# A two-layer hybrid decoder trunk in split fp32: key and query projections paired like the feed-forward, and the order of work at the head and at the stage borders

## The reference

```python
for l in range(DEPTH):          # DEPTH = 2
    x = x + 0.5 * rmsnorm(swiglu(rmsnorm(x, g1), w_gate, w_up, w_down), g2)      # D_FF = 2816
    x = x + rmsnorm(hybrid_mixer(rmsnorm(x, g3), cos, sin, w_in, ...), g4)       # retention + gated linear attention
    x = x + rmsnorm(memory_cross_attn(rmsnorm(x, g5), rmsnorm(mem, g6), w_q, w_kv, w_o), g7)
    x = x + 0.5 * rmsnorm(swiglu(rmsnorm(x, g8), w_gate2, w_up2, w_down2), g9)

def memory_cross_attn(h, mem_n, w_q, w_kv, w_o):       # 4 heads of 256, 256 memory tokens
    q = (h @ w_q).reshape(bsz, t, XA_HEADS, XA_DH)
    k, v = jnp.split(mem_n @ w_kv, 2, axis=-1)
    s = jnp.einsum('bthd,bmhd->bhtm', q, k) * (XA_DH ** -0.5)
    return (softmax(s) @ v) @ w_o
```

## Time and profile before

| | |
|---|---|
| median of three executions | 1198.43 us |
| the profiled execution's own time | 1198.46 us |
| its span, first to last instruction | 1196.6 us |
| PE busy | 1187.7 us, 99% |
| weight loads (PEld), beside PE | 1017.4 us, 85% |
| DVE busy | 821.2 us, 69% |
| ACT busy | 693.0 us, 58% |
| GpSimd busy | 147.5 us, 12% |
| mean granted TensorE clock | 0.999 |
| DMA | 217.84 MB, 182 GB/s over the span |

### The profile page before, as it was taken

How to read it: one execution, slowest core, us unless ns; L and a number is a source line. 1 busy time by engine, 2 the same in 40 slices (tenths; PEclk the granted TensorE clock), 3 DMA queues, 4 the chain that set the end, 5 groups by cost and what they waited for, 6 DMA issues and landing times.

```text
span 1196.6 us, 17899 instructions
## 1 busy us (share of the span) xinstructions
PE 1187.7 (99%) x6492; PEld 1017.4 (85%) x6492; DVE 821.2 (69%) x1258; ACT 693.0 (58%) x1190; POOL 147.5 (12%) x230
## 2 busy tenths in 40 slices
PE   9999999999999999999999999999999999999998
PEld 8788888779898888888888888887899988888886
DVE  6766645788667677775487875477887676778752
ACT  7655445756565566664466764376566565666641
POOL 3000002573100100000000000025531001000000
PEclk9999999999999999999999999999999999999999
DMA  9656565454444455556465555554545444555550
GB/s 371 224 183 217 182 205 186 150 211 142 163 172 162 138 193 184 203 187 209 152 207 181 201 198 194 193 200 139 172 140 178 161 151 159 185 205 177 192 178 36
DMA packets 33063, 217.84 MB, mean 182 GB/s; under 512 B 3920, under 2 KB 4176, under 8 KB 9440
## 3 DMA queue, kind: packets, MB, share of 16 engines
q1 hardware_dynamic: 32848, 216.77, 53.0%
q10 hardware_dynamic: 144, 0.13, 0.0%
HBM read 215.84 MB, written 1.05 MB: 181 GB/s over the span
## 4 chain that ended last, share of the span: by engine, by line
PE 95%; DMA 2%; DVE 1%; ACT 1%; issue 1%; POOL 0%; SPq 0%; POOLq 0%; DVEq 0%; ACTq 0%
PE acc L558 21%; PE acc L559 21%; PE acc L560 21%; PE acc L716 16%; PE acc L717 9%; PE tb L619 2%; DMA raw<-in_gu 2%; PE mb L795 1%; DVE w_lo L1466 1%; ACT w_hi L1049 1%; PE mb L560 0%; PE mb L559 0%; PE mb L558 0%; PE mb L882 0%; PE mb L866 0%
## 5 line engine op out<-in xcount | busy, mean ns | idle before, releaser
L1466 DVE SCALAR_TENSOR_TENSOR w_lo<-raw,first,w_hi 128x512 fp32r<-128x512 f32 x576 | 413.4, 772 | 87.4 <-ACT w_hi L1049 85.8
L1049 ACT ACTIVATE w_hi<-raw,first 128x512 fp32r<-128x512 f32 x568 | 367.6, 714 | 112.5 <-PE acc L717 47.0
L716 PE MATMUL acc<-xT,w_hi 128*128 128x512 f32 x864 | 300.2, 392 | 0.0
L717 PE MATMUL acc<-xT,w_lo 128*128 128x256 f32 x864 | 242.5, 281 | 0.0
L558 PE MATMUL acc<-w_hi,xT 128*128 128x512 f32 x592 | 235.8, 398 | 1.0 <-DVE xT L1472 0.9
L559 PE MATMUL acc<-w_lo,xT 128*128 128x512 f32 x592 | 231.2, 391 | 0.0
L560 PE MATMUL acc<-w_hi,xT 128*128 128x512 f32 x592 | 231.1, 390 | 0.0
L716 PEld LDWEIGHTS acc<-xT,w_hi 128*128 128x128 f32 x864 | 161.8, 187 | 35.1
L1458 DVE TENSOR_TENSOR w_lo<-raw,w_hi 128x1024 fp32r<-128x1024 f32 x112 | 124.6, 1146 | 90.0 <-ACT w_hi L1043 89.4
L717 PEld LDWEIGHTS acc<-xT,w_lo 128*128 128x128 f32 x864 | 163.8, 190 | 0.1
L1043 ACT ACTIVATE w_hi<-raw 128x1024 fp32r<-128x1024 f32 x112 | 106.6, 991 | 95.7 <-PE acc L560 79.1
(11 more groups left out here) (219 smaller groups left out, 1441.0 us busy)
## 6 DMA issues: line engine op xcount, KB each, us to landing
raw<-in_gu SPq DMA_DIRECT2D x86, 1024.0 KB, 5.0
raw<-in_down SPq DMA_DIRECT2D x32, 1024.0 KB, 4.9
raw<-in_in SPq DMA_DIRECT2D x24, 1024.0 KB, 4.9
raw<-in_kv SPq DMA_DIRECT2D x16, 1024.0 KB, 5.0
raw<-in_down SPq DMA_DIRECT2D x16, 768.0 KB, 4.2
raw<-in_out SPq DMA_DIRECT2D x8, 1024.0 KB, 4.9
raw<-in_q SPq DMA_DIRECT2D x8, 1024.0 KB, 5.0
raw<-in_o SPq DMA_DIRECT2D x8, 1024.0 KB, 4.9
```

The costliest lines, as they stand in the source:

```text
L716: pe.matmul(o[:, :], w_hi[:, slot, kk, c:c + P], xT[:, :, k, :], start=k == 0, stop=False)
L717: mm = pe.matmul(o[:, TOK:2 * TOK], w_lo[:, slot, kk, c:c + P], xT_hi[:, k, :], start=False, stop=k == KD - 1)
L1049: act.activation(w_hi[:, slot, k, :], raw[:, slot, k, :], ACT.Copy, scale=gains[:, ds(g, 1)]).then_inc(s_hi, 1)
L1466: dve.scalar_tensor_tensor(w_lo[:, slot, k, :], raw[:, slot, k, :], gains[:, ds(g, 1)], w_hi[:, slot, k, :].bitcast(F32), ALU.mult, ALU.su ...
```

## The change

Four parts.

1. Key and query projections use the feed-forward's form: for each k one matmul of 512 (`w_hi` by both inputs) and one of 256 (`w_lo` by the high input). A pass fills two banks, so each of the four chunks takes one accumulator number more (Q_OUT to Q_AV shift), and a bank's next use comes two passes later. `column_low` (ACT) copies the right halves of both banks to `col_sum`, `column_sum` (DVE) adds the left halves and frees the banks, `column_hi` (ACT) and `column_lo` (DVE) split the sum. The `split_hi` and `split_lo` around them are cut in two parts each.
2. PE waits for `s_hi` ahead of a k and for `s_lo` only ahead of the matmul that reads `w_lo`, in token passes, the first chunk and the column passes; in token passes and the first chunk the matmul with `w_lo` comes last.
3. Head: 12 warm-up matmuls for 18, the first weights in six pieces and the input in four, in another order; sine and cosine and a first tanh ahead of the second chunk's `split_hi`; `tanh(1, 0)` and `gated(1, 0)` ahead of chunk 2's first half, `tanh(1, 1)` and `gated(1, 1)` ahead of its second.
4. Borders of phases 2 and 3: ACT's `x_square` ahead of both `split_hi`, `x_hi` ahead of the second; DVE's `x_norm` ahead of both `split_lo`, `x_lo` ahead of the second; the transposes of phase 3 one k earlier.

```diff
-WARM = 18
-FIRST = ((0, 0, 1), (0, 1, 2), (0, 2, 4), (1, 0, 2), (1, 2, 4))
-XT_IN = ((0, 2), (2, 4), (4, 8))
+WARM = 12
+FIRST = ((0, 0, 1), (0, 1, 2), (0, 2, 3), (0, 3, 4), (1, 0, 2), (1, 2, 4))
+XT_IN = ((0, 2), (2, 4), (4, 6), (6, 8))
...
+            def three_moving(o, st_hi, st_lo, mv_hi, mv_lo, first, last, low=None):
+
+                pe.matmul(o, st_hi, mv_hi, start=first, stop=False)
+                pe.matmul(o, st_lo, mv_hi, start=False, stop=False)
+                if low is not None:
+                    pe.wait_ge(s_lo, low)
+                return pe.matmul(o, st_hi, mv_lo, start=False, stop=last)
...
-                            pe.wait_ge(s_lo, 4 * half_no(l, ci, h) + 4 * x_ci + step)
+                            low = 4 * half_no(l, ci, h) + 4 * x_ci + step
+                            pe.wait_ge(s_hi, low)
...
             def column_pass(l, ci, t, src, mid=None):
...
+                    q = col_q(ci, t)
+                    wait_acc(l, q, mt)
+                    o = acc_of(l, q, mt)
...
                             if t == 0 and mt == 0:
-                                pe.wait_ge(s_lo, 4 * half_no(l, ci, h) + k + 1)
-                            mm = three(acc_of(l, q, t)[:, mt * 256:mt * 256 + 256], w_hi[:, slot, k, c:c + P],
-                                       w_lo[:, slot, k, c:c + P], src_hi[:, 4 * h + k, :], src_lo[:, 4 * h + k, :],
-                                       h == 0 and k == 0, h == 1 and k == 3)
+                                pe.wait_ge(s_hi, low)
+                            pe.matmul(o[:, :], w_hi[:, slot, k, c:c + P], src[:, :, 4 * h + k, :],
+                                      start=h == 0 and k == 0, stop=False)
+                            if t == 0 and mt == 0:
+                                pe.wait_ge(s_lo, low)
+                            mm = pe.matmul(o[:, TOK:2 * TOK], w_lo[:, slot, k, c:c + P], src[:, 0, 4 * h + k, :],
+                                           start=False, stop=h == 1 and k == 3)
...
             def boundary(l, phase, q, ci):
 
                 y_square(l, phase, q, 1, 0)
-                split_hi(l, ci + 1, 0)
                 if phase == 0:
+                    split_hi(l, ci + 1, 0)
                     x_hi(l, phase + 1, 0)
-                x_square(l, phase + 1, 0)
-                if phase == 2:
-                    y_square(l, phase, q - 1, 0, 1)
-                split_hi(l, ci + 1, 1)
-                if phase != 0:
+                    x_square(l, phase + 1, 0)
+                    split_hi(l, ci + 1, 1)
+                else:
+                    x_square(l, phase + 1, 0)
+                    split_hi(l, ci + 1, 0)
+                    if phase == 2:
+                        y_square(l, phase, q - 1, 0, 1)
                     x_hi(l, phase + 1, 0)
+                    split_hi(l, ci + 1, 1)
...
                     tanh(0, 0, None)
                     tanh(0, 1, None)
+                    tanh(1, 0, None)
                     split_hi(l, c0 + 2, 0)
+                    tanh(1, 1, None)
                     split_hi(l, c0 + 2, 1)
-                    tanh(1, 0, None)
-                    tanh(1, 1, None)
...
+            def column_low(l, ci, t):
+                n = col_no(l, ci, t)
+                if n % 8 == 0:
+                    act.wait_ge(s_hss, l * 4 + 4)
+                if n >= 2:
+                    act.wait_ge(s_clo, n - 1)
+                for mt in range(2):
+                    act.wait_ge(s_acc, chunk_pass_no(l, ci, 2 * t + mt) + 1)
+                    ins = act.activation(col_sum[n % 2][:, mt, :], acc_of(l, col_q(ci, t), mt)[:, TOK:2 * TOK],
+                                         ACT.Copy)
+                ins.then_inc(s_clow, 1)
+
+            def column_hi(l, ci, t, dst):
+                q = col_q(ci, t)
+                for mt in range(2):
+                    act.wait_ge(s_accf[bank(l, q, mt)], acc_uses(l, q) + 1)
+                act.activation(dst, col_sum[col_no(l, ci, t) % 2], ACT.Copy).then_inc(s_chi, 1)
...
             def attention(l):
-                copy_out(l, Q_K1, 0, kT_hi[:, 4:6, :], s_khi)
+                column_low(l, C_K1, 0)
                 x_hi(l, 2, 0)
+                column_hi(l, C_K1, 0, kT_hi[:, 4:6, :])
                 split_hi(l, C_Q, 1)
                 x_hi(l, 2, 1)
                 x_square(l, 2, 1)
...
             def boundary(l, phase, q, ci):
                 y_gain(l, phase, q, 1, 0)
                 x_update(l, phase, q, 0)
+                if phase != 0:
+                    x_norm(l, phase + 1, 0)
                 split_lo(l, ci + 1, 0)
-                if phase == 0:
-                    x_lo(l, phase + 1, 0)
-                else:
-                    x_norm(l, phase + 1, 0)
                 if phase == 2:
                     y_gain(l, phase, q - 1, 0, 1)
+                x_lo(l, phase + 1, 0)
                 split_lo(l, ci + 1, 1)
-                if phase != 0:
-                    x_lo(l, phase + 1, 0)
...
+            def column_sum(l, ci, t):
+                n = col_no(l, ci, t)
+                q = col_q(ci, t)
+                dve.wait_ge(s_clow, n + 1)
+                for mt in range(2):
+                    dve.tensor_tensor(col_sum[n % 2][:, mt, :], acc_of(l, q, mt)[:, 0:TOK], col_sum[n % 2][:, mt, :],
+                                      ALU.add).then_inc(s_accf[bank(l, q, mt)], 1)
...
             def attention(l):
+                column_sum(l, C_K1, 0)
                 x_lo(l, 2, 0)
                 k_lo(l, 1, 0)
                 split_lo(l, C_Q, 1)
                 x_lo(l, 2, 1)
-                split_lo(l, C_Q + 1, 0)
+                split_lo(l, C_Q + 1, 0, parts=(0,))
+                column_sum(l, C_K1, 1)
+                split_lo(l, C_Q + 1, 0, parts=(1,))
                 k_lo(l, 1, 1)
```

More of the change, by code:

```diff
@@ L96 @@
 Q_K0 = Q_IN + 6
-Q_OUT = Q_K0 + 1
+Q_OUT = Q_K0 + 2
 Q_K1 = Q_OUT + 2
-Q_Q = Q_K1 + 1
-Q_V = Q_Q + 2
+Q_Q = Q_K1 + 2
+Q_V = Q_Q + 4
 Q_AV = Q_V + 2
@@ L108, in by_feature_ffn @@
     return (l, f) != (0, 0)
+COLUMN_CHUNKS = (C_K0, C_K1, C_Q, C_Q + 1)
 def feature_chunks_done(l, ci):
-    return sum(min(max(ci - C_FFN[f] - TOK_CH, 0), FEAT) for f in range(2) if by_feature_ffn(l, f))
+    ffn = sum(min(max(ci - C_FFN[f] - TOK_CH, 0), FEAT) for f in range(2) if by_feature_ffn(l, f))
+    return ffn + sum(1 for c in COLUMN_CHUNKS if c < ci)
 LAST_CHUNK = {Q_FFN[f] + j: C_FFN[f] + j for f in range(2) for j in range(FU)}
@@ L395, in last_pass_no @@
         def last_pass_no(l, ci):
-            feature = any(TOK_CH <= ci - C_FFN[f] < FU and by_feature_ffn(l, f) for f in range(2))
+            feature = ci in COLUMN_CHUNKS or any(TOK_CH <= ci - C_FFN[f] < FU and by_feature_ffn(l, f) for f in range(2))
             return chunk_pass_no(l, ci, 3 if feature else 1)
@@ L582, in token_pass @@
                         sl = slice(t * P, t * P + P)
-                        mm = three(o[:, :], src_hi[:, ks, sl], src_lo[:, ks, sl], w_hi[:, slot, k, :],
-                                   w_lo[:, slot, k, :], first and h == 0 and k == 0, last and h == 1 and k == nk - 1)
+                        mm = three_moving(o[:, :], src_hi[:, ks, sl], src_lo[:, ks, sl], w_hi[:, slot, k, :],
+                                          w_lo[:, slot, k, :], first and h == 0 and k == 0,
+                                          last and h == 1 and k == nk - 1, low)
                         if t == 1 and k == nk - 1 and h == 0:
@@ L681, in first_chunk @@
                         for k in range(4):
-                            pe.wait_ge(s_lo, 4 * h + k + 1)
+                            ks = 4 * h + k
+                            pe.wait_ge(s_hi, ks + 1)
+                            if k % 2 == 0:
+                                pe.wait_ge(s_tev, ks // 2 + 1)
                             for t in range(TT):
-                                ks = 4 * h + k
-                                if t == 0 and k % 2 == 0:
-                                    pe.wait_ge(s_tev, ks // 2 + 1)
                                 sl = slice(t * P, t * P + P)
-                                mm = three(acc[0][t][:, :], xT_hi[:, ks, sl], xT_lo[:, ks, sl], w_hi[:, h, k, :],
-                                           w_lo[:, h, k, :], ks == 0, ks == KD - 1)
+                                o = acc[0][t][:, :]
+                                pe.matmul(o, xT_hi[:, ks, sl], w_hi[:, h, k, :], start=ks == 0, stop=False)
+                                pe.matmul(o, xT_lo[:, ks, sl], w_hi[:, h, k, :], start=False, stop=False)
+                            pe.wait_ge(s_lo, ks + 1)
+                            for t in range(TT):
+                                sl = slice(t * P, t * P + P)
+                                mm = pe.matmul(acc[0][t][:, :], xT_hi[:, ks, sl], w_lo[:, h, k, :], start=False,
+                                               stop=ks == KD - 1)
                                 if ks == KD - 1:
@@ L1429, in _ @@
             first_weights(2)
+            first_weights(3)
```

(16 more changed lines are left out.)

142 lines of the change are left out of this document (87 added, 55 removed).

## The result

The changed kernel takes 1191.38 us (median of six executions, 1190.95 to 1191.56), the kernel before beside it 1198.44: a ratio of 0.9941, 95% interval 0.9931 to 0.9952. The forecast was 1190.9. The profiled execution took 1191.56 us with a span of 1189.8, so its span is 6.8 us shorter than before's 1196.6.

The account below looks back on a forecast made before the run. PE was taken as the bound nearly everywhere. Terms -3.3 + 0.2 - 1.25 - 1.1 - 1.25 + 0.15 - 1.0 = -7.55 us against 1198.46 gave 1190.9 us; range 1188.3 to 1195.0, about 0.85.

Parts of the forecast that it names:

- Columns: Key and query passes: a pair costs 0.346 us against 0.359 for three short matmuls, saving 3.3 us over 16 passes.
- Rival C: Key and query passes: the new pair costs what three short matmuls cost, giving 1194.2 us; chance 0.04.
- The wait at the first Q pass: PE's first query pass: DVE's extra sum uses up 0.43 us of cover, adding 0.1 us in each layer, +0.2 us.
- Rival B: Key and query stretch: ACT and DVE become late, at `x_lo(2, 1)` and for the scores, giving 1193 to 1195 us; chance 0.13.
- Split waits: Passes with t = 0: about 470 second waits on PE cost at most 2 ns each; taken as nothing.
- Rival D: Inside a k, the `s_lo` wait keeps the next weight load from running ahead: 42 us lost, 1233 us; chance 0.04.
- Head: Kernel start and chunk 2: earlier first product saves 1.25 us, removed wait in chunk 2 saves 1.1, together 2.35 us.
- The stop at k = 2: First chunk's third k: weights' high part ready at 9.0 to 9.7 us for a need at 9.2; no wait taken.
- Rival A: Kernel start: pieces land late or clumped, so the head gives 0.5 instead of 2.35 us, total 1192.8; chance 0.14.
- In chunk 2 the wait: Chunk 2's second hidden block: earlier tanh removes PE's 0.99 us wait ahead of the transposes, saving 1.1 us.
- Borders: phase 2: Border behind phase 2, both layers: waits of 0.24 us ahead of the transposes and 0.25 behind go, saving 1.0 us in all.
- Phase 3: Phase 3's border in layer 0: both first-tile waits go, saving 1.25 us, while the second tile adds 0.15 us.

Follow-up runs that it names:

- head and split waits alone: The kernel before with only the head's changes and the split waits of token passes and first chunk, without columns and borders: 1195.60 us, ratio 0.9979.
- the nudge: The changed kernel with small unread matmuls (32 columns in layer 0, 64 in layer 1) ahead of four key and query pass entries per layer: 1192.64 us, ratio 0.9954.

## Why the prediction was right, and where its terms were off

**Columns: right in kind, half in size.** The step that was mis-sized is "the new pair is the feed-forward's, 0.346 us". It took eight pairs of one feed-forward chunk for the price of the form. The form has two prices, 0.3467 and 0.3533, and 104 of 128 pairs pay the second: 104 x 0.0066 = 0.69 us in a layer, which takes the 1.65 to 0.96; 0.98 was measured. My bounds for this term (nothing and 3.3 us) held it. Rival C was half true. DVE and ACT grew by 9.8 and 10.1 us, where I had 13 and 12. The saving of 1.96 us in both layers lies midway between my 3.3 and the estimate of 0.6 by the Trainium skill's formula (the same page as above, Back-to-back issue gap).

**The wait at the first Q pass: 0.2 us that did not come.** The step was that DVE's added `column_sum` uses the cover up. It took 0.75 us and lay whole in the 1.12 us of idle time ahead of `x_lo(2, 0)`; `x_lo(2, 1)` starts 333.13 - 330.29 = 2.84 us sooner than before, and PE's first Q pass 334.84 - 331.90 = 2.94. Of the 0.43 us of cover 0.33 are left. Rival B has nothing in the list of waits.

**Split waits: nothing, as taken.** Rival D is refuted: in passes with t = 0 the starts stay 0.227 us apart, and without the waits of the token passes no mark behind the head moves. Without them PE stopped 0.5 us once in the head, in the one execution profiled; the medians show nothing of it.

**Head: 2.40 against 2.35, with two terms that offset.** That it came so near is luck: the terms are off by 0.3 and 0.46 us and the executions differ by as much. The first product came 1.58 us sooner instead of 1.27, since the clock was up by the first k. The stop at k = 2, taken as nothing, cost 0.46. I had put its weights' high part at 9.0 to 9.7 us against a need at 9.2, and taken no wait; it was ready at 9.37 against a need at 9.05. The input piece, which I had not costed, was late by the same amount. So chunk 1 began at 17.79 us and not at 17.4. Rival A's cause was real, at a quarter of its price (0.46 of 1.85 us). In chunk 2 the wait went as described, 1.23 us for 1.1.

**Borders: phase 2 gave 0.66 us a layer for 0.5.** I had priced both stops at their idle time, 0.24 + 0.25 us, and they cost 0.17 more: a stop also lengthens the distances behind it, in the kernel before by 0.06 us at the transposes behind the first and by 0.10 over the six products behind the second. Phase 3 gave 1.09 for 1.10 by two errors that offset. By the same neglect the two stops of the first tile were worth 1.45 us and not 1.25 (the marks up to the second tile's transposes gain 0.92 + 0.28, its stop of 0.26 included), and the second tile took back 0.26 + 0.10 us, its stop and the distances behind it, and not 0.15.

Together: 1.34 too much for the columns, less the 0.2 of a wait that did not come, 0.05 for the head and 0.33 for phase 2, leave 1.34 - 0.2 - 0.05 - 0.33 = 0.76; 7.55 - 6.86 = 0.69 is missing at the last matmul. The step that failed in size is the columns' price, and half of its error was made good by others of the other sign; that part of the near hit, 1191.38 for 1190.9, is luck.

**Left open.** What sets a pair's pace when a pass is entered. The runs show that it is set there and holds, not by which distance. Also why the head's pieces land when they do: in the profiled executions of the changed kernel, of head and split waits alone and of the nudge the second input piece, issued at the same time, landed at 7.98, 6.84 and 6.68 us.

## What to carry to other kernels

Price an instruction form from more than one place of the trace before counting it into a sum; a difference of 2% in the distance of starts, over the 840 pairs behind the feed-forwards' transposes, was worth more than any one part of this change. When a wait is moved away, read the queues of both helper engines from the update on, since the next late thing is decided by what stands ahead of each of the three short instructions (here the square, the norm and `x_lo`) and by what is pushed behind them. A stop of PE costs its idle time and, in the places measured here, 0.06 to 0.1 us behind it.

## What the runs showed of the hardware

A stream of matmuls of 512 and 256 columns in turn has two steady paces, 0.3467 and 0.3533 us for a pair, both at the upper clock level, with the same operands and no wait. What stands at a break (where the transposes are, or two matmuls of 64 columns more) selects between them, and the pace holds over hundreds of pairs. It made 5.3 us of 1191 here. The shorter pace has the same two distances in each pair, 0.230 and 0.117 us; the longer one repeats in threes, with 0.241, 0.236 and 0.233 from the 512 to the 256.

Two stops of PE of 0.24 and 0.25 us cost 0.66 us together in phase 2. Behind the stop at 604.94 the eight transposes and the first product behind them took 0.84 + 0.33 us, and without a stop (the changed kernel at 31.39) 0.80 + 0.31.
